# State-space stage of a two-layer hybrid block: decay sums loaded as rows, floors on VectorE, one exponential a chunk, no work for GpSimd

## The reference, cut to what matters

```python
a_cs = jnp.moveaxis(jnp.cumsum(dtc * a.reshape(G, HG), axis=2), 2, -1)
xdt = xc * dtc[..., None]
cb = jnp.einsum("bclgn,bcsgn->bcgls", cc, bc)
y_diag = jnp.einsum("bcgls,bcghls,bcsghp->bclghp", cb, exp_segsum(a_cs), xdt)
decay_to_end = jnp.exp(a_cs[..., -1:] - a_cs)
states = jnp.einsum("bclgn,bcghl,bclghp->bcghpn", bc, decay_to_end, xdt)
chunk_decay = jnp.exp(a_cs[..., -1])
# over the chunks: carry * chunk_decay + states
y_off = jnp.einsum("bclgn,bcghpn,bcghl->bclghp", cc, prev, jnp.exp(a_cs))
y = y_diag + y_off + xs * d_skip
g = y * silu(z);  g = g * rsqrt(mean(g * g, per group) + eps) * w
```

## Time and profile before

| what | us |
|---|---|
| median of 3 runs | 3471.3 (3470.49 to 3471.34) |
| the profiled execution's own time | 3469.94 |
| its span, first to last instruction | 3468.1 |
| first state-space stage in it, 2140.88 to 2321.67 | 180.8 |
| second state-space stage, 3094.05 to 3274.42 | 180.4 |
| PE, DVE, ACT, POOL busy over the span | 3187.7, 1530.2, 1038.9, 1080.5 |

### The profile page before, as it was taken

One profiled execution on the slowest core, in us unless ns is written; L12 is line 12 of the kernel. 1 busy time (PEld: TensorE's weight loads), 2 busy tenths in 40 slices (PEclk: granted clock), 3 DMA queues, 4 the chain that ended last, 5 costly groups with the idle time before them and its releaser, 6 DMA issues. The chain is left out here.

```text
span 3468.1 us, 49486 instructions
## 1 busy us (share of the span) xinstructions
PE 3187.7 (92%) x21000; PEld 2545.8 (73%) x21016; DVE 1530.2 (44%) x2122; ACT 1038.9 (30%) x1822; POOL 1080.5 (31%) x698
## 2 busy tenths in 40 slices
PE   5998799777999998989999998879899999988798
PEld 3885489665888877878777776658787777766587
DVE  3999645424222224341244343871312443438713
ACT  3012333313222222222244343530122444435401
POOL 2443022103333324323333332333233333323342
PEclk8999899898999999999999999989999999999899
DMA  5113200222111111222121224004221212240142
GB/s 198 49 49 118 102 4 4 77 87 74 48 48 48 48 30 61 97 79 75 49 79 49 67 92 154 11 34 143 84 76 48 80 49 68 91 157 8 36 144 76
DMA packets 210596, 250.71 MB, mean 72 GB/s; under 512 B 9280, under 2 KB 164032, under 8 KB 207968
## 3 DMA queue, kind: packets, MB, share of 16 engines
q1 hardware_dynamic: 199584, 208.02, 18.5%
q10 hardware_dynamic: 10240, 37.75, 2.8%
q0 software_dynamic: 576, 2.10, 0.2%
HBM read 199.60 MB, written 46.14 MB: 71 GB/s over the span
## 5 line engine op out<-in xcount | busy, mean ns | idle before, releaser
L1875 PE MATMUL PS<-x_high_sb,w_high_sb 128*128 128x512 f32 x1312 | 530.1, 404 | 0.0
L1875 PE MATMUL PS<-x_high_sb,w_low_sb 128*128 128x512 f32 x1312 | 518.2, 395 | 0.0
L1875 PE MATMUL PS<-x_low_sb,w_high_sb 128*128 128x512 f32 x1312 | 517.4, 394 | 0.0
L1875 PEld LDWEIGHTS PS<-x_high_sb,w_high_sb 128*128 128x128 f32 x1312 | 247.0, 188 | 76.1 <-issue 23.9
L1875 PEld LDWEIGHTS PS<-x_high_sb,w_low_sb 128*128 128x128 f32 x1312 | 246.9, 188 | 57.8
L360 PE MATMUL PS<-h_high_sb,up_high_sb 128*128 128x512 f32 x704 | 275.0, 391 | 13.5 <-POOL up_low_sb L1445 13.5
L1875 PEld LDWEIGHTS PS<-x_low_sb,w_high_sb 128*128 128x128 f32 x1312 | 247.3, 189 | 52.3
L360 PE MATMUL PS<-h_low_sb,up_high_sb 128*128 128x512 f32 x704 | 274.6, 390 | 0.0
L360 PE MATMUL PS<-h_high_sb,up_low_sb 128*128 128x512 f32 x704 | 274.6, 390 | 0.0
L1495 DVE SCALAR_TENSOR_TENSOR z_sb<-PS,cols_sb,z_sb 128x1023 f32<-128x1023 f32 x88 | 112.8, 1282 | 348.9 <-ACT z_sb L1476 342.5
L2112 DVE CUSTOM_DVE_ANT_0 scores_sb<-PS,alibi_sb,sinks_sb 128x256 f32<-128x256 f32 (+1 forms) x256 | 104.4, 464 | 341.8 <-PE PS L1893 341.6
(11 more groups left out here) (409 smaller groups left out, 6461.8 us busy)
## 6 DMA issues: line engine op xcount, KB each, us to landing
w_raw_sb<-w_in SPq DMA_DIRECT2D x102, 512.0 KB, 3.9
up_raw_sb<-w_up SPq DMA_DIRECT2D x44, 512.0 KB, 3.9
ada_slots_sb<-ada_w SPq DMA_DIRECT2D x16, 1024.0 KB, 5.5
w_raw_sb<-w_out SPq DMA_DIRECT2D x64, 256.0 KB, 2.8
xbc<-staged_sb ACTq DMA_DIRECT2D x24, 512.0 KB, 2.6
down_raw_sb<-w_down SPq DMA_DIRECT2D x44, 256.0 KB, 2.6
xbc_sb<-xbc SPq DMA_DIRECT2D x2, 5376.0 KB, 19.1
attn<-HT_sb ACTq DMA_DIRECT2D x8, 1024.0 KB, 4.9
```

The costliest lines, as they stand in the source:

```text
L1875: last = pe.matmul(PS[:, bank, :], a[:, n % 2, k], b[:, k, cols], start=k == 0 and a is WH and b is HH, stop=k == KT - 1 and a is WL)
```

## The change

Between the last projections of a layer and its state-space stage nothing is added but a store: StepSizes turns NA with TensorE, so that each (chunk, head) is one row of 128 tokens, ScalarE copies it and stores it to device memory (rows_d, 64 KB).

In state_space the rows R of TensorE and their masks are gone. SP loads, for each chunk, its 16 rows into every partition (1 MB, three slots). They hold minus the running sum of the later token l. VectorE subtracts the running sum's own column from them and takes the larger of the result and 0, head by head (floors, 16 instructions of 128x128). ScalarE takes one exponential of minus that over all 16 heads. The triangle that makes the other pairs zero is multiplied once into C times B (masked), and VectorE multiplies it in, eight heads at a time (weigh).

GpSimd has no work. VectorE makes both scaled inputs straight from X in PSUM, the second with DE times DT, which is multiplied once for all chunks. The skip term is a matmul of x with a diagonal, summed into the same banks as the products within the chunk. The inverse root is computed on 4 x 32 partitions for 64 columns and spread over the partitions by small matmuls (spread). The state, the inputs and B have two buffers each. The order of each queue is written out by hand.

```diff
+        pe.transpose(self.m.PS[:, 3, 0:TT * SH], self.NA[:], self.m.const("ident")).then_inc(self.s.turned, 1)
...
+        act.wait_ge(s.turned, 1)
+        nc.scalar.copy(self.tmp[:, 0], self.m.PS[:, 3, 0:TT * SH]).then_inc(s.ex, 1)
+        act.wait_ge(s.ex, 4)
+        act.dma_start(self.rows_d, self.tmp[:, 0]).then_inc(s.row_out, 16)
...
-                    pe.wait_ge(step.s.ex, 3)
+                    pe.wait_ge(step.s.ex, 4)
...
+            def rows(c):
+                sp.dma_start(E[:, c % SLOTS], rows_d[c * SH:(c + 1) * SH].unsqueeze(0).to_broadcast([P, SH, P])
+                             ).then_inc(row_in[c % SLOTS], 16)
+
+            rows(0)
+            sp.dma_start(XB[:, :, 0:P], xbc_d[:, :, 0:P].rearrange("k p t -> p k t")).then_inc(s.x_in0, 16)
+            sp.dma_start(skip[:], d_skip.to_broadcast([P, SH])).then_inc(s.skip_in, 16)
+            rows(1)
+            sp.dma_start(XB[:, :, P:T], xbc_d[:, :, P:T].rearrange("k p t -> p k t")).then_inc(s.x_in1, 16)
+            rows(2)
             sp.dma_start(ZS[:], gate_d.rearrange("k p t -> p k t")).then_inc(s.z_in, 16)
+            for c in range(SLOTS, TT):
+                sp.wait_ge(s.yd, c - SLOTS + 1)
+                rows(c)
...
+            def from_state(c):
+                pe.wait_ge(s.st_out, c)
+                pe.wait_ge(s.y, c)
+                for g in range(SG):
+                    last = pe.matmul(PS[:, 2 + g, :], XB[:, KT + SG + g, cols(c)], S[:, c % 2, g * GW:(g + 1) * GW],
+                                     start=True, stop=True)
+                last.then_inc(s.yo, 1)
...
+            def within(c):
+
+                pe.wait_ge(s.xdt, c + 1)
+                if c:
+                    pe.wait_ge(s.yo_out, c)
+                else:
+                    pe.wait_ge(s.small, 2)
+                for q in range(KT):
+                    pe.matmul(PS[:, 2 + q // 4, (q % 4) * P:(q % 4 + 1) * P], XB[:, q, cols(c)], SKIP[:, q],
+                              start=q % 4 == 0, stop=False, skip_group_check=True)
+                for h in range(SH):
+                    if h % 8 == 0:
+                        pe.wait_ge(s.masked, 2 * c + h // 8 + 1)
+                    last = pe.matmul(PS[:, 2 + h // 8, (h % 8) * HD:(h % 8 + 1) * HD], E[:, c % SLOTS, h],
+                                     XDT[:, c % 2, h * HD:(h + 1) * HD], start=False, stop=True, skip_group_check=True)
+                last.then_inc(s.yd, 1)
+
+            def y_turned(c):
+                pe.wait_ge(s.y, c + 1)
+                if c:
+                    pe.wait_ge(s.normed, c)
...
+            def square_sums(c):
+                pe.wait_ge(s.squared, c + 1)
+                if c:
+                    pe.wait_ge(s.rooted, c)
+                for q in range(KT // SG):
+                    for r in range(4):
+                        g, a = r // 2, r % 2
+                        last = pe.matmul(PS[32 * r:32 * r + 32, 5, 0:HD], m.const("ones")[:, 0:32],
+                                         SQ[:, g * (KT // SG) + q, a * HD:(a + 1) * HD], start=q == 0,
+                                         stop=q == KT // SG - 1)
+                last.then_inc(s.ss, 1)
+
+            def spread(c):
+
+                pe.wait_ge(s.inverse, c + 1)
+                for a in range(2):
+                    for g in range(SG):
+                        r = slice(32 * (2 * g + a), 32 * (2 * g + a) + 32)
+                        last = pe.matmul(PS[:, 6 + g, a * HD:(a + 1) * HD], m.const("headpick")[r, 0:P], RS[r, c % 2],
+                                         start=True, stop=True)
+                    last.then_inc(s.spread, 1)
+                    if a == 0:
+                        pe.wait_ge(s.spread, 2 * c + 1)
...
+            b_and_cb(0)
+            x_turned(0)
+            for c in range(TT):
+                if c >= 2:
+                    spread(c - 2)
+                if c:
+                    from_state(c)
+                if c < TT - 1:
+                    to_state(c)
+                if c:
+                    y_turned(c - 1)
+                within(c)
+                if c + 1 < TT:
+                    if c == 0:
+                        pe.wait_ge(s.x_in1, 16)
+                    b_and_cb(c + 1)
+                    x_turned(c + 1)
+                if c:
+                    square_sums(c - 1)
+            spread(TT - 2)
+            y_turned(TT - 1)
+            square_sums(TT - 1)
+            spread(TT - 1)
...
+            def exps(c):
+                e = E[:, c % SLOTS]
+                act.wait_ge(s.floored, SH * (c + 1))
+                nc.scalar.activation(e, e, ACT.Exp, scale=-1.0).then_inc(s.exps, 1)
...
+            move(0)
+            exps(0)
             for c in range(TT):
                 if c:
+                    square(c - 1)
+                if c + 1 < TT:
+                    move(c + 1)
+                    exps(c + 1)
+                if c:
+                    root(c - 1)
+            square(TT - 1)
+            root(TT - 1)
...
+            def floors(c):
+                dve.wait_ge(row_in[c % SLOTS], 16 * (c // SLOTS + 1))
+                for h in range(SH):
+                    e, at = E[:, c % SLOTS, h], c * SH + h
+                    v.tensor_scalar(e, e, NA[:, at:at + 1], 0.0, ALU.subtract, ALU.max).then_inc(s.floored, 1)
+
+            def weigh(c):
+                dve.wait_ge(s.exps, c + 1)
+                dve.wait_ge(s.cb, c + 1)
+                for g in range(SG):
+                    e = E[:, c % SLOTS, 8 * g:8 * g + 8]
+                    cb = BC[:, c % 2, (2 + g) * P:(3 + g) * P].unsqueeze(1).to_broadcast([P, SH // SG, P])
+
+                    v.tensor_tensor(e, e, cb, ALU.mult).then_inc(s.masked, 1)
+
+            def inputs(c):
+                dve.wait_ge(s.x, c + 1)
+                if c >= 2:
+                    dve.wait_ge(s.yd, c - 1)
+                v.tensor_tensor(by_head(XDT[:, c % 2]), heads(X_ST), wide(DT, c), ALU.mult).then_inc(s.xdt, 1)
+                v.tensor_tensor(by_head(XDE[:, c % 2]), heads(X_ST), wide(DE, c), ALU.mult).then_inc(s.xde, 1)
...
             for c in range(TT):
+                y = Y[:, c % 2]
+                if c:
+                    dve.wait_ge(s.yo, c)
+                    if c >= 2:
+                        dve.wait_ge(s.g, c - 1)
+                    v.tensor_tensor(by_head(y), heads(YO_YD), wide(EI, c), ALU.mult).then_inc(s.yo_out, 1)
+                    if c < TT - 1:
+                        v.tensor_tensor(by_head(S[:, (c + 1) % 2]), by_head(S[:, c % 2]), wide(CD, c), ALU.mult
+                                        ).then_inc(s.grown, 1)
+                if c + 1 < TT:
+                    floors(c + 1)
+                if c >= 2:
+                    normalise(c - 2)
+                if c < TT - 1:
+                    dve.wait_ge(s.st, c + 1)
+                    after = S[:, (c + 1) % 2]
+                    if c:
+                        dve.wait_ge(s.grown, c)
+                        v.tensor_tensor(after, after, PS[:, X_ST, :].rearrange("p a b -> p (a b)"), ALU.add
+                                        ).then_inc(s.st_out, 1)
...
                 if c:
                     gate(c - 1)
...
+                dve.wait_ge(s.yd, c + 1)
                 if c:
+                    dve.wait_ge(s.yo_out, c)
+                    v.tensor_tensor(by_head(y), by_head(y), heads(YO_YD), ALU.add).then_inc(s.y, 1)
...
+                if c + 1 < TT:
+                    masked(c + 1)
+                    inputs(c + 1)
+                    weigh(c + 1)
+                if c:
+                    invert(c - 1)
+            normalise(TT - 2)
             gate(TT - 1)
+            invert(TT - 1)
             normalise(TT - 1)
```

More of the change, by code:

```diff
@@ L1710, in __init__ @@
         self.tmp = alloc(m, ctx, "dt_tmp", [P, 5, TT * SH])
-        self.s = phase(m, "par_in ab e chain sums acs last ex")
+        self.s = phase(m, "par_in ab e chain sums acs last ex turned row_out")
         self.sums, self.ends = m.PS[:, 0, 0:TT * SH], m.PS[:, 2, 0:TT * SH]
@@ L2195, in state_space @@
-        s = phase(m, "rows_in x_in0 x_in1 z_in pe act dve pool masks m_ready chain y_sum squared inverse normed")
+        s = phase(m, "skip_in row_in0 row_in1 row_in2 x_in0 x_in1 z_in b x yo st yd g ss spread kept cb moved small xdt xde "
+                     "yo_out st_out y gate grown floored exps masked squared rooted inverse normed")
+        row_in = [s.row_in0, s.row_in1, s.row_in2]
         block = ctx.enter_context(nc.Block())
-        order = [("B", "act", 7, 1), ("R0", "act", 4, 1), ("X", "act", 0, 2), ("R1", "act", 5, 1),
-                 ("R2", "act", 4, 1), ("R3", "act", 5, 1), ("G", "dve", 0, 2),
-                 ("YO", "dve", 2, 2), ("ST", "dve", 6, 2), ("SS", "act", 4, 1), ("YD", "dve", 0, 2)]
@@ new lines, in b_and_cb @@
+            def b_and_cb(c):
+                if c:
+                    pe.wait_ge(s.moved, c)
+                    pe.wait_ge(s.cb, c)
+                for g in range(SG):
```

(42 more changed lines are left out.)

230 lines of the change are left out of this document (62 added, 168 removed).

## The result

The changed kernel took 3538.57 us (median of 4 runs, 3535.53 to 3542.55), the kernel before 3471.32 beside it: ratio 1.0195, 95% interval 1.0177 to 1.0212. It is slower by 67 us, where 75 were forecast (3545, range 3486 to 3588).

What follows compares the result with a forecast made beforehand. Before, a loop over TensorE, one copy and GpSimd (20.6 us a chunk); after, a TensorE-VectorE relay with slow clock (27.4). Stage 218.4 against 180.8, +37.6; two stages +75 on 3469.9: 3545 us, range 3486 to 3588.

Steps and rivals of the forecast that it cites:

- The two waits: In TensorE's queue, the spread waits for the inverse and y's transposes for the normalise, each ahead of a needed product.
- the relay: In middle chunks TensorE and VectorE take strict turns: 23.9 us, 27.4 with slow clock; chance 0.50 with clock dips.
- The signs that were named: Trace after: chunks of 27 us, VectorE idle 3 and 4 us, TensorE idle 5 us before transposes, clock under 0.8.
- The rival on the faster side: TensorE's 9.9 us in a chunk lie beside VectorE's work; cycle 15.5 us, kernel 3400 us; chance 0.05.
- The legs of a chunk: Four turns of TensorE and VectorE in a middle chunk: 3.3, 6.7, 6.6 and 7.3 us, 23.9 at full clock.
- the clock's share: TensorE at half clock after idles adds 2.6 us to leg C and 0.9 to leg A, giving 27.4 a chunk.
- The loop of the kernel before: A middle chunk's 20.6 us runs over TensorE, ScalarE's copy of X and GpSimd's three multiplies, 6.7 us.
- The ends of the stage: Start until 24.3 us, chunk 1 14.2, chunk 2 27.2, chunk 7 23.1, and 20 us after the last y's start.
- just in time: At the stage's start the rest of xbc lands at about 24 us, as chunk 0's within products end at 24.3.
- The rival of late rows: Row broadcasts slower than 407 GB/s make chunk 1 start late: 5 us a layer, 3555 us; chance 0.04.
- the tail: Stage's end, from the last y's start: 16.5 us of work plus 3.5 at 1.2 GHz, 20 against 14.05 before.
- Before the stage: The added transpose, copy and store per layer cost zero, being covered; without that cover 0.4 us a layer.

Runs made afterwards that it cites:

- Moving either alone: Changed kernel with TensorE's spread put after the state's products, 3478.18 us; or with VectorE's normalise put ahead of the floors, 3484.98 us.
- the clock held: Changed kernel in its own order, with 20 unneeded matmuls a chunk ahead of the spread and 16 ahead of the transposes: 3493.03 us.
- both moves: Changed kernel with the spread after the state's products and the normalise ahead of the floors: 3448.90 us, ratio 0.9934 to the kernel before.
- the fastest version: Changed kernel with both moves, unneeded matmuls, and chunk 1 of xbc and z's first two chunks loaded ahead of the rest: 3421.00 us.

## Why the prediction was right, point by point

**The sign and its cause.** The two waits were named before the run as the place of the relay. Moving either alone gives back 60 and 54 us, both together 90. The signs that were named came: chunks of 27 us, clock 0.75, TensorE idle 4.5 us ahead of the transposes. VectorE's two idles were forecast as 3 and 4 us and are 5.3 each; with the clock held they are 2.95 and 4.08. The rival on the faster side, where the legs of TensorE lie beside VectorE's work, had its mechanism right for another order: that order is the one of both moves. The change has it not.

**The legs of a chunk**, from the two timelines of the chunk:

| leg | forecast | measured | why they differ |
|---|---|---|---|
| A, VectorE's end to its restart | 3.3 + 0.9 clock | 5.3 | the state product ran wholly at half clock, 3.78, not 2.8 |
| B, VectorE to the normalise's end | 6.7 | 6.6 | |
| C, TensorE to y | 6.6 + 2.6 clock | 8.7 | the clock was back within the skip products (3.23) |
| D, y to the inverse's end | 7.3 | 7.1 | |
| chunk | 27.4 | 27.7 | |

Chunks 3 to 6 took 27.4 us on average (109.6 for four), just the forecast. The size of the clock's share was 3.5 us a chunk in the sum, and 4.2 with the gaps filled (27.4 less 23.24). A likely cause of leg A's miss is a term mis-sized elsewhere: the square sums were put at 2.0 to 3.7 us and took 0.65, so TensorE was idle for 5.08 us ahead of leg A and not for 2 to 3.

**The loop of the kernel before.** The prediction read it as TensorE, one copy and GpSimd. That was half of it: with the wait for GpSimd's last multiply gone the loop fell by 0.7 us and not by 2.3, because the squares behind VectorE's slowed multiplies came almost as late. The forecast didn't rest on this, for it took the 20.6 us as measured.

**The floors.** 3.22 us for sixteen, forecast 3.2: the row of 0.227 us less the overlap of 0.08 plus 0.05 for the pointer was sound. One lasts 0.279 and the next starts after 0.20. The Trainium skill's estimate ("VectorE: DVE Perf Modes", The TRN2 errata), 2.0 us for sixteen, is too low by 1.2; its warning about the fixed part of small tiles agrees with the cut floors, which cost 2.07 us a chunk more for the same columns.

**The ends of the stage** came out near only in their sum, by luck, for two large misses have opposite signs, and this is where the 9.5 us lie by which the two stages were over-forecast (65.7 against 75). The start took 22.6 us instead of 24.3. Chunk 1 took 18.4 instead of 14.2. The step that failed there is "just in time": the rest of xbc was forecast to land at about 24 and landed at 25.5, but y of chunk 0 began at 22.6, and behind the load stood a B at half clock, ScalarE's copy and X, so that VectorE's inputs began 6.2 us after y where 1.8 was forecast. The rival of late rows named 5 us a layer and the wrong load: the rows came in time, xbc didn't, and in the run with xbc cut z was late behind it. With both loads cut chunk 1 takes 14.7, close to the forecast. Chunk 2 took 27.75, forecast 27.2. Chunk 7 took 21.3 instead of 23.1, and the tail 13.6 instead of 20. The timeline of TensorE shows why:

```profile
2338.24 1.06 PE L2288 MATMUL PS<-consts_sb,y_sb 128*128 128x128 f32 x8 [2.53 <-DVE HT_sb L2427]
2339.14 1.95 PE L2274 MATMUL PS<-skip_diagonal_sb,xbc_sb 128*128 128x128 f32 x16
...
2349.10 1.94 PE L2288 MATMUL PS<-consts_sb,y_sb 128*128 128x128 f32 x8 [1.41 <-DVE HT_sb L2427]
2353.45 1.08 PE L2299 MATMUL PS<-gated_squares_sb,consts_sb 128*32 128x64 f32 x32 [2.40 <-ACT gated_squares_sb L2358]
```

In chunk 7 (first two rows) the clock held behind an idle of 2.53 us: 1.06 for the transposes, not 1.94, and the skip products took 1.95. In the tail three terms were too large: the normalise of chunk 6 ended 4.3 us after the start of the last y, where 6.4 was forecast; the square sums cost 1.08 us at half clock and not 3.0; and of the 3.5 us of clock price on top only about 0.7 came, at the transposes (1.94, forecast 1.2). The terms sum: -1.7 + 4.2 + 0.5 - 1.8 - 6.4 = -5.2 in the first layer.

**Before the stage** at nothing: between the two stages 772.4 us passed before and 772.7 after, so the transpose, the copy and the store are hidden, as forecast.

**What stays open.** Why the clock holds behind an idle of 2.53 us in chunk 7 and of 1.95 with the normalise early, and is half behind 2.49 with both moves, isn't settled. In the kernel before with GpSimd's order changed it differs even behind the same idle: 2.96 us each time, then square sums of 2.02 us in some chunks and 3.35 to 3.76 in others. No run varied the length of one idle in steps. The start of the first stage, which differs by up to 6 us between executions with the same code ahead of it, wasn't looked into.

## What to carry to other kernels

Work out the order as a relay: for each wait in a queue, write down what stands behind it and who waits for that; two orders of the same instructions differed here by 90 us. When a hand-off can't be hidden, put the needed product ahead of the wait and the free work (here the floors) behind the hand-off, and reckon with a price for the clock where TensorE is idle: 45.5 us here, though not every idle cost it. A wait that is removed is worth only the distance to the next one: look for the second bound before counting on a gain.

## What the runs showed that was not expected

- Thirty-two short matmuls, which write 32 partitions each (128*32, 64 columns), took 0.65 us at full clock, 0.02 us each, and 1.08 at half; the 32 products of line 2286, 128*128 with the same 64 columns, take 3.68.
- 13 unneeded matmuls a chunk (26 instructions, 3.3 us of TensorE's time) belong to the fastest version, and 36 a chunk made the change itself 45.5 us faster.
- GpSimd made two of VectorE's multiplies of 1024 columns take 4.37 us for 2.36, but three of 512 columns 6.15 for 2.04: in the chunks shown each ended about 1.1 and 0.55 us after a GpSimd multiply ended.
- Removing one wait made the kernel before 28 us slower; in its trace products of 3.68 us take 6.93, at half clock.
